# Moving the norms and transposes of an encoder's first token tiles under the matmuls of its last ones

## What is computed

```python
for l in range(DEPTH):                                   # DEPTH = 2
    mod = (c_act @ w_ada[l] + b_ada[l])[:, None, :]      # 6 * 1024 columns
    sh_a, sc_a, g_a, sh_m, sc_m, g_m = jnp.split(mod, 6, axis=-1)
    h = x * (1.0 + sc_a) + sh_a
    proj = h @ w_in[l]
    ...                                                  # three attention mixers give y_a, y_b, y_c
    y = jnp.concatenate([heads_to_seq(y_a), heads_to_seq(y_b), heads_to_seq(y_c)], -1) @ w_o[l]
    x = layer_norm(ALPHA * x + (1.0 + g_a) * y, ln1_g[l], ln1_b[l])
    h = x * (1.0 + sc_m) + sh_m
    y = jnp.square(jax.nn.relu(h @ w1[l])) @ w2[l]       # D_FF = 4096
    x = layer_norm(ALPHA * x + (1.0 + g_m) * y, ln2_g[l], ln2_b[l])
return x
```

## Time and profile before

| | us |
|---|---|
| median of 3 runs (1447.02 to 1449.18) | 1447.26 |
| the profiled execution | 1448.38 |
| its span, first to last instruction | 1446.6 |
| PE busy | 1324.9 (92%) |
| DVE busy | 1011.6 (70%) |
| ACT busy | 598.5 (41%) |
| POOL busy | 339.9 (23%) |

### The profile page before, as it was taken

The page is one execution under the profiler, slowest core; times in us unless marked ns, Lnnn a source line. Parts: engine busy times, 40 slices in busy tenths (PEclk is TensorE's granted clock), DMA queues, the critical chain, the costliest instruction groups (busy, mean ns, idle before and its releaser), DMA issues.

```text
span 1446.6 us, 19841 instructions
## 1 busy us (share of the span) xinstructions
PE 1324.9 (92%) x6696; PEld 1120.0 (77%) x6696; DVE 1011.6 (70%) x1650; ACT 598.5 (41%) x1212; POOL 339.9 (23%) x409
## 2 busy tenths in 40 slices
PE   4998998899899999999969899879989999999992
PEld 2897877787788888888869877768778888888882
DVE  6768788877678465565785878978674855454478
ACT  0356478851432222222244647878152232222221
POOL 0022066630125000000321406856010700000024
PEclk9999989999999999999989999999999999999996
DMA  8864600005233343344246462010423333333331
GB/s 284 302 203 165 204 14 14 27 22 173 76 119 128 117 129 113 100 129 147 79 154 202 155 212 72 1 39 1 145 87 96 95 99 97 94 98 98 95 102 58
DMA packets 87577, 164.38 MB, mean 114 GB/s; under 512 B 7960, under 2 KB 18584, under 8 KB 87504
## 3 DMA queue, kind: packets, MB, share of 16 engines
q1 hardware_dynamic: 86976, 161.34, 34.4%
q10 hardware_dynamic: 528, 2.10, 0.4%
HBM read 159.21 MB, written 4.19 MB: 113 GB/s over the span
## 4 chain that ended last, share of the span: by engine, by line
PE 68%; DVE 17%; DMA 6%; ACT 4%; issue 3%; POOL 2%; SPq 0%; ACTq 0%; DVEq 0%; POOLq 0%
PE bank L1325 21%; PE bank L1326 21%; PE bank L1327 21%; DMA ada_w<-in_w_ada 2%; DVE pt_lo L1076 2%; PE bank L1354 2%; DVE ada_sum L839 2%; PE bank L1492 2%; DMA slab_raw<-in_w_in 1%; DVE smax L1063 1%; DVE X L1104 1%; DVE stats L1107 1%; DVE tmp L1101 1%; DVE k_lo L1037 1%; DVE acc L1246 1%
## 5 line engine op out<-in xcount | busy, mean ns | idle before, releaser
L1325 PE MATMUL bank<-hT_hi,slab_hi 128*128 128x512 f32 x576 | 224.5, 390 | 1.2 <-ACT kB L658 1.2
L1156 DVE TENSOR_TENSOR slab_lo<-slab_raw,slab_hi 128x512 fp32r<-128x512 f32 x240 | 183.0, 815 | 60.1 <-ACT slab_hi L793 51.8
L1327 PE MATMUL bank<-hT_hi,slab_lo 128*128 128x512 f32 x576 | 224.1, 389 | 0.0
L1326 PE MATMUL bank<-hT_lo,slab_hi 128*128 128x512 f32 x576 | 224.1, 389 | 0.0
L1325 PE MATMUL bank<-slab_hi,h_hi 128*128 128x512 f32 x512 | 200.1, 391 | 2.8 <-ACT mod_a L810 2.8
L1327 PE MATMUL bank<-slab_hi,h_lo 128*128 128x512 f32 x512 | 199.3, 389 | 0.0
L1326 PE MATMUL bank<-slab_lo,h_hi 128*128 128x512 f32 x512 | 199.2, 389 | 0.0
L1325 PE MATMUL bank<-slab_hi,hT_hi 128*128 128x384 f32 (+3 forms) x448 | 151.6, 338 | 4.0 <-DVE hT_lo L1084 2.8
L1327 PE MATMUL bank<-slab_hi,hT_lo 128*128 128x384 f32 (+3 forms) x448 | 150.9, 337 | 0.0
L1326 PE MATMUL bank<-slab_lo,hT_hi 128*128 128x384 f32 (+3 forms) x448 | 150.8, 337 | 0.0
L839 DVE SCALAR_TENSOR_TENSOR ada_sum<-ada_w,c_col,ada_sum 128x512 f32<-128x512 f32 x168 | 129.5, 771 | 16.2 <-DMA ada_w<-in_w_ada 13.1
(11 more groups left out here) (198 smaller groups left out, 2601.2 us busy)
## 6 DMA issues: line engine op xcount, KB each, us to landing
slab_raw<-in_w SPq DMA_DIRECT2D x256, 256.0 KB, 2.7
ada_w<-in_w_ada SPq DMA_DIRECT2D x48, 1024.0 KB, 5.4
slab_raw<-in_w_in SPq DMA_DIRECT2D x48, 192.0 KB, 5.3
slab_raw<-in_w_o SPq DMA_DIRECT2D x32, 256.0 KB, 2.9
slab_raw<-in_w_in SPq DMA_DIRECT2D x16, 256.0 KB, 5.3
band<-bias_rows SPq DMA_DIRECT2D x8, 448.0 KB, 3.2
slab_raw<-in_w_in SPq DMA_DIRECT2D x16, 144.0 KB, 3.7
X<-in_x SPq DMA_DIRECT2D x1, 2048.0 KB, 10.1
```

The costliest lines, as they stand in the source:

```text
L1156: dve.tensor_tensor(slab_lo[:, slot, :], slab_raw[:, slot, :], f32(slab_hi[:, slot, :]), ALU.subtract).then_inc(slab_lo_done, 1)
L1325: pe.matmul(dst, a_hi, w_hi, start=first, stop=False)
L1326: pe.matmul(dst, a_hi, w_lo, start=False, stop=False)
L1327: return pe.matmul(dst, a_lo, w_hi, start=False, stop=last)
```

## The change

The reference is computed as before; what moves is when, where and in which pieces.

- **Output projection, second half** (`wo_second`): token tiles 0 and 1 over all eight slabs, then tiles 2 and 3. The 16 transposes of tiles 0 and 1 stand between slabs 5 and 6 of the second pair.
- **First FF product of group 0** (`first_group`): 256 tokens a matmul instead of 512, first pair over the slabs, then the second pair, with the 16 transposes of tiles 2 and 3 in two portions of eight around slab 7 of the first pair. The first chunk of the input projection (`first_chunk`) is divided in the same way.
- **Norm**: POOL does the whole of it in place of DVE's shift and ACT's scaling: 1/sqrt, then one `tensor_scalar` (subtract mean, multiply) for each half tile. ACT writes `hT_hi` directly from PSUM and `tmp` with a second activation; DVE makes `hT_lo` only.
- **FF**: groups 6 and 7 are not added to `acc`; their second products accumulate in all eight banks. X scaled plus `acc` times gate is made by DVE in step 6, ahead of the squares of group 7 (16 instructions, and in layer 0 four small ones that set up the next layer's modulation). The last group's second product goes tiles 0 and 1 first, both halves, then tiles 2 and 3; in layer 0 layer 1's 16 transposes stand inside it, in layer 1 tile 2 comes before tile 3.
- **Modulation**: the two blocks with the MLP gate leave the output projection for FF steps 0 and 1, the four of the next layer go to steps 2 to 5, a whole block to a step. ACT now takes them before it splits the next four slabs, not behind.
- **Output**: eight stores of 256 KB. POOL finishes tiles 0 and 1 half by half (L556 to L559), DVE tiles 3 and 2 with two fused instructions for each half.
- Banks are grouped 0, 1, 4, 5 and 2, 3, 6, 7 for the output projection and FF; small buffers move in SBUF.

The core of the diff:

```diff
+                def normalise(n):
+                    for t in range(TT):
+                        rstd_of(n, t)
+                        pool.wait_ge(rstd_ready, l * 8 + 4 * n + t + 1)
+                        for j in range(2):
+                            xs = X[:, t, 512 * j:512 * j + 512]
+                            pool.tensor_scalar(xs, xs, mv[:, t, MV_MEAN:MV_MEAN + 1], mv[:, t, MV_RSTD:MV_RSTD + 1],
+                                               ALU.subtract, ALU.mult).then_inc(xhat_ready, 1)
...
+                    ht_low(job, 0, l_next)
+                    ht_low(job, 1, l_next)
+                    half_done()
+                    at2 = take(src(2), n, 2, 1)
+                    all_done()
+                    at3 = take(src(3), n, 3, 1)
+                    split(first + 4, width, l_next)
+                    ht_low(job, 2, l_next)
+                    add_to_x(n, 2, 1, at2)
...
+                def first_group():
+                    def columns(p, ks, cs):
+                        for k in ks:
+                            pe.wait_ge(ht_ready, l * 32 + 16 + 8 * p + k + 1)
...
+                    columns(0, range(3), (0, 1))
+                    pe.wait_ge(evac_dve, l * D_LAYER + d_before("wo1") + 4)
+                    columns(0, range(3), (2, 3))
+                    columns(0, range(3, 7), range(4))
+                    transpose_x("lns", 1, range(4))
+                    columns(0, range(7, 8), range(4))
+                    transpose_x("lns", 1, range(4, 8))
+                    columns(1, range(8), range(4))
...
-                    add_up(banks(JOB["w1"] + 1 + u + 1), 0, gm, base_at + (RING + PRE + 20))
+                    add_up(ff_sets(u)[1], 0, gm, base_at + (RING + PRE + 20))
...
+                for t in range(TT):
+                    at = [scale_acc(t, j) for j in range(2)]
+                    for j in range(2):
+                        base_of_x(t, j, at[j])
```

More of the change, by code:

```diff
@@ L818, in _ @@
                     act.activation(slab_hi[:, k, :], slab_raw[:, k, :], ACT.Copy).then_inc(slab_hi_done, 1)
-                for t in range(TT):
-                    normalise(1, t)
+                if l < DEPTH - 1:
+                    norm_entry("lnp", 0, 0, 384, l + 1)
         @block.vector
@@ L1093, in _ @@
                                           ALU.subtract).then_inc(v_ready, 1)
[L1095 to L1105 removed]
+                gated = [0]
@@ L1106, in residual, with stats_of @@
+                def stats_of(t, j):
                     settle()
-                    step(dve.bn_stats(stats[:, t, 6 * j:6 * j + 6], xs))
+                    step(dve.bn_stats(stats[:, t, 6 * j:6 * j + 6], X[:, t, 512 * j:512 * j + 512]))
+                def residual(src, n, t, j):
+                    add_to_x(n, t, j, take(src, n, t, j))
+                    stats_of(t, j)
                 def moments(t):
-                    wait_apart(dve, dve_step, now())
+                    settle()
@@ new lines, in _, with scale_acc @@
+                for k in range(4):
+                    split_at(k, base_at + (PRE + 16 + k + 1))
+                dve.wait_ge(x_ready, l * 8 + 8)
+                dve.wait_ge(evac_act, relu_base + 5 * LATE)
+                dve.wait_ge(evac_dve, l * D_LAYER + D_LAST)
+                gated[0] = D_LAST
+                def scale_acc(t, j):
+                    a = acc[:, t, 512 * j:512 * j + 512]
+                    step(dve.tensor_tensor(a, a, gate[:, 1, 512 * j:512 * j + 512], ALU.mult))
+                    return now()
@@ new lines, in wo_second @@
+                def wo_second():
+                    free_after("wo1")
+                    for p in range(2):
+                        for k in range(8):
+                            kt = WO_ORDER[k]
+                            if p == 0:
+                                slab_ready(l * SLABS + 8 * WO1 + k + 1)
+                            for t in (2 * p, 2 * p + 1):
+                                ins = three(banks(JOB["wo1"])[t][:, :], hT_hi[:, kt, t * P:(t + 1) * P],
+                                            hT_lo[:, kt, t * P:(t + 1) * P], slab_hi[:, k, :], slab_lo[:, k, :],
+                                            k == 0, k == 7)
+                                if k == 7 and t in (1, 2):
+                                    ins.then_inc(wo_tile, 1)
+                            if p == 1:
+                                ins.then_inc(slab_free, 1)
+                                if k == 5:
+                                    free_after("lnr")
+                                    transpose_x("lnr", 1, range(8))
@@ new lines, in mlp_step @@
+                    pe.wait_ge(evac_act, relu_at + 4)
+                    if mod is not None:
+                        pe.wait_ge(ada_half, mod * 2 + 2)
+                        if wide:
+                            pe.matmul(h1_set[3][:, :], ones[:, :], ada_sum[:, 0, :], start=True, stop=True
+                                      ).then_inc(mod_ready, 1)
+                        else:
+                            mod_cols(h1_set[3], ada_sum[:, 0, :])
+                    w2_half(h1_set, gm, u, 1, at + (PRE + 20), None if mod is None else relu_at + 5, more)
@@ new lines, in _, with last_group @@
+                mlp_step(GROUPS - 2, 0, relu_base + 4 * (GROUPS - 2) + LATE + (AHEAD if l < DEPTH - 1 else 0), more=True)
+                def last_group(tiles, j, f):
+                    slot = 4 * j + f
+                    slab_ready(l * SLABS + SLABS - 8 + slot + 1)
+                    for t in tiles:
+                        ins = three(ff_bank(t, j)[:, :], h2_hi[:, 1, f, t * P:(t + 1) * P],
+                                    h2_lo[:, 1, f, t * P:(t + 1) * P], slab_hi[:, slot, :], slab_lo[:, slot, :],
+                                    False, f == 3)
+                        if f == 3 and j == 1 and tiles == (2, 3) and t == 2:
+                            ins.then_inc(ff_tile, 1)
+                    if tiles[-1] == 3:
+                        ins.then_inc(slab_free, 1)
+                    elif f == 3:
+                        ins.then_inc(ff_tile, 1)
```

665 lines of the change are left out of this document (369 added, 296 removed), and 2 rows, old and new, of the table JOBS.

## The result

The changed kernel takes 1460.32 us (median of 7 runs, 1455.38 to 1465.16), the kernel before 1447.25 (7 runs, 1446.69 to 1449.18). The ratio is 1.0088, 95% interval 1.007 to 1.0106. The forecast was 1414 and a range of 1403 to 1431: wrong in size and in sign. The profiled span is 1458.6 us, 12.0 more than before.

A forecast was written before the change was run, and what follows sets the result against it. PE was taken as the bound, busy 92% of the span, with gains only where it stands. Terms -12.6 - 11.9 - 10.9 + 1.0 + 2.3 - 1.0 = -33.1 us gave 1415.3, stated as 1414 us, range 1403 to 1431.

The forecast's parts named there:

- From wo1 to FF: Handover from output projection to FF, both layers: gaps shrink to transposes, narrow matmuls and short waits; saves 6.1 and 6.5 us.
- POOL contends with DVE: Handovers, tail and step 6: POOL's wide work slows DVE's passes; +19.6 us, 1434 us, chance 0.20.
- Between the layers: Handover from layer 0 to layer 1: of 19.4 us only transposes and 3.7 us of waits stay; saves 11.9 us.
- The tail: From the last matmul to the end: 16.0 us remain, 20.6 with a clash on every pass; saves 10.9 us.
- FF and step 6: FF stages: gate blocks less a dropped wait add 1.0 us; 16 new DVE passes in step 6 add 2.3.
- The opening and attention: Program start: 16 transposes leave the front, most taken back by ACT's pace, -1.0 us; layer 1's attention 0.
- Rival 1: Handovers, tail and step 6: DVE becomes the bound beside POOL's wide work; +19.6 us, 1434 us, chance 0.20.
- Rival 2: wo1 handovers: group 0's narrow product starts as late as before, those gaps gain nothing; 1427 us, chance 0.07.
- Rival 3: Handovers and step 6: everything is covered, no waits and step 6 free; 1403 us, chance 0.09.
- Rival 4: Transposes stay at 0.20 us each wherever they stand; 7.7 us more, 1422 us, chance 0.03.
- Rival 5: Narrow matmuls and transposes: weight loads bound them at 0.20 us, slower than before; +41 us, 1455 us, chance 0.03.
- PE's matmul distance off 0.227 anywhere: Sign that the forecast is wrong: PE's matmuls start at a distance other than 0.227 us anywhere.

The follow-up runs named there:

- e2: The changed kernel with POOL's norm using add and mult on a negated mean instead of subtract and mult; 1427.64 us, ratio to before 0.9863.
- e4: e2 with POOL doing the first halves of both tiles of a pair, then the second halves; 1423.91 us, ratio to before 0.9851.
- e9: e8 with the 16 transposes inside wo1 one slab later, behind the seventh instead of the sixth; 1419.12 us, ratio to before 0.9803.
- e6: e2 with layer 0's opening not in pairs: all transposes first, then the first product over four tiles; 1429.32 us, ratio to before 0.9888.
- e1: The changed kernel with 48 extra POOL instructions, twelve forms on a scratch tile, in layer 1's FF; span 1461.1 us, a single run.
- e5: e2 with the tail redivided: ACT normalises five half tiles, POOL does gain and bias of five, DVE of three; 1429.64 us, ratio to before 0.9882.
- e8: e4 with DVE doing all eight half tiles of the tail and POOL only the four 1/sqrt; 1421.66 us, ratio to before 0.9821.

## Why the prediction was wrong, point by point

**The step that failed** is a price. Under "From wo1 to FF" it says that POOL needs "0.7 for each half tile". The row is attention's `tensor_scalar`, mult and mult; the changed kernel's is subtract and mult. Same engine, same name, same shape, other operation: 2.07 against 0.72. The before kernel had no `subtract` on POOL, so no row had this price and it could only be bounded; the nearest rows of 512 columns on POOL were 0.7 and 1.74, four half tiles at the upper one are 7 us in place of 2.8, and even that lies below the 2.07 measured. Instead the forecast treated it as read, in the handovers and in the tail, and no rival held it: "POOL contends with DVE" had its chance, "this instruction is slow by itself" had none. The sign of the miss hangs on it: with the one form exchanged the kernel is 1.4% faster than before. Of the 46 us between the 1414 forecast and the 1460.3 measured, this exchange gives back 33; the other 13 are spread over the terms below and over the opening and attention, which no term explains.

**What followed from it** had no price in the forecast, which let PE run at full rate behind its new waits. A wait of PE of 4.4 us cost more than 4.4: with the slow transposes and matmuls behind it the place in layer 0 lost 7.7 us against full-speed distances, that between the layers 6.6 for a wait of 3.3.

**Against e2, term by term**, which is the test of the rest (e2's span is 22.0 below before's, the forecast sum was 33.1):

- *wo to FF*: forecast -6.1 and -6.5, e2 -4.0 and -5.9. Right in kind. The wait was 2.3 us where 0.3 to 1 was forecast. Part of that is POOL's order, both halves of tile 0 ahead of tile 1's first: with the other order (e4) it was two waits of 0.84, and with the transposes a slab later as well (e9) 0.6 in all.
- *Between the layers*: forecast -11.9, e2 -9.3. The handover's waits were as forecast (1.4 for `hT_lo`, 1.4 for X, forecast 3.7 with all). Behind them PE waited 2.8 us for slabs before the stage ended (1.2, 0.3, 0.7 and 0.6), where the kernel before waited for none: about the 2.6 us that are missing. That the first product, which holds its slots through both passes, made them late is shown for the opening (e6) and only argued here; e4, with the same product, had 1.4 us of such waits in place of 2.8. The prediction said that a slab "still ends before its use"; it looked at FF's narrow product alone, not at this one.
- *The tail*: forecast -10.9, e2 -7.7. The mechanism was forecast (1/sqrt behind POOL's halves, DVE's passes at 1.7 beside POOL), but clashes were put on three passes and struck more, on DVE's additions into X as well. Its upper end, 20.6 us behind the last matmul with a clash on every pass, held e2's 19.3; the changed kernel's 22.5 lay above it.
- *FF and step 6*: forecast +3.3, measured +1.3 over the two FF stages. Step 6 cost a wait of 0.4 us in layer 0 (0.3 in the changed kernel) and none in layer 1 for the 2.3 forecast; the gate's blocks and the dropped wait of 2.8 us were sized about right.
- *The opening and attention*: forecast -1.0 and 0, e2 +0.9 and +2.7, the changed kernel +2.8 and +0.8. The first matmul did come 4.3 us earlier in the changed kernel, and nothing of it was left at `wo`. These stages vary by 2.4 and 4.5 us between the traces of kernels that don't differ in them, so the other differences here are not read.

**Rivals.** Rival 1 (DVE bounds the handovers) fell: 2.0 us of `hT_lo` waits in all. What is right in it is the contention, in the tail and in e1, and there it matters what POOL does. DVE's `slab_lo` passes, two SBUF inputs each, beside POOL's one-input `subtract` (L562) and beside its two-input `tensor_tensor` (L568) in e1:

```profile
1194.26 9.20 POOL L562 TENSOR_SCALAR prob<-prob,mone 128x512 f32<-128x512 f32 x4
1199.19 2.49 DVE L1250 TENSOR_TENSOR slab_lo<-slab_raw,slab_hi 128x512 fp32r<-128x512 f32 x4
...
1230.03 6.84 DVE L1250 TENSOR_TENSOR slab_lo<-slab_raw,slab_hi 128x512 fp32r<-128x512 f32 x4
1231.31 6.72 POOL L568 TENSOR_TENSOR prob<-prob 128x512 f32<-128x512 f32 x4
```

The first four passes took 0.68 us each while POOL's `subtract` was running all along; the last four took 1.75 to 1.78 each. The Trainium skill, page "SBUF — State Buffer", section "SBUF: two separate sides", says that a DVE instruction with two SBUF inputs contends with a GpSimd instruction that reads SBUF; the trace agrees, with 1.74 us for a pass of e5 beside POOL and 0.75 for the same in e8. It does not bear out the lock for a whole instruction that the prediction took from that section: the first four passes above ran at full speed beside POOL's `subtract`, of which the last took 2.9 us where the others took 2.0, and beside the other one-input forms of e1 no two-input pass of DVE took more than 1.15.

Rival 2 (half of it lands) gave 1427, and e2 measured 1427.6. That is a coincidence of numbers: the `wo1` gaps, which it had at nothing, brought 9.9 us in e2. Rival 3 (everything covered) fell with the 8.4 us of waits for X and `hT_lo` that e2 kept. Rival 4 (transposes stay at 0.20) was right only behind a stand. Eight of them inside the matmul stream of the changed kernel's opening took 0.11 us each at a granted clock of 1.00, near the prediction's 0.12. That goes against the page of the Trainium skill that the prediction cites for rival 4, and the measurement decides. (The 0.09 that the prediction read from four rows is 0.11 as well, from start to start.) The row:

```profile
55.02 1.03 PE L1478 MATMUL bank<-ident,X 128*128 128x128 f32 x8
```

Rival 5 fell: the narrow matmuls stood 0.12 apart wherever PE had its full clock. They stood 0.21 apart from 386.46 to 388.60, behind a stand of 3.86 us, at a granted clock of 0.50. So "PE's matmul distance off 0.227 anywhere", one of the prediction's signs of being wrong, did come, with the clock and not with weight loads as its cause. That the kernel could be slower had 0.03, all of it on rival 5; it came by another road.

## What to carry to other kernels

A price is that of an instruction with its operations, not of its name and shape: if the trace doesn't show the pair of operations on that engine, treat it as unknown, and run the form alone before building a schedule on it. Work put under matmuls is hidden only if it ends before PE asks for it, so order it as PE takes it. A share of DVE's two-input work on SBUF given to POOL can be worth nothing, as it was in this tail.
